# FFN up projection: two halves of the activations side by side in one 512-wide matmul per weight tile

## The reference

```python
def _swiglu(x, w1, w2):
    gt, up = jnp.split(x @ w1, 2, axis=-1)      # w1: 1024 x 5632
    return (jax.nn.silu(gt) * up) @ w2          # w2: 2816 x 1024

x = _layer_norm(DN_ALPHA * x + 0.5 * _swiglu(x, ffn1_w1[l], ffn1_w2[l]), ln1_g[l], ln1_b[l])
mix = _token_mix(x, ...)
x = _layer_norm(DN_ALPHA * x + mix, ...)
x = _layer_norm(DN_ALPHA * x + 0.5 * _swiglu(x, ffn2_w1[l], ffn2_w2[l]), ln3_g[l], ln3_b[l])
```

## Time and profile before

| | |
|---|---|
| time, median of 3 runs | 3143.65 us (3134.18 to 3158.1) |
| span of the profiled execution | 3151.0 us |
| PE busy | 2905.6 us, 92% |
| PE weight loads busy | 2683.1 us, 85% |
| POOL busy | 1948.4 us, 62% |
| ACT busy | 1181.7 us, 38% |
| DVE busy | 947.6 us, 30% |
| data moved | 491.20 MB, 156 GB/s on average |

### The profile page before, as it was taken

The page is one execution under the profiler, slowest core; times in us unless marked ns, Lnnn a source line. Parts: engine busy times, 40 slices in busy tenths (PEclk is TensorE's granted clock), DMA queues, the critical chain, the costliest instruction groups (busy, mean ns, idle before and its releaser), DMA issues.

```text
span 3151.0 us, 53968 instructions
## 1 busy us (share of the span) xinstructions
PE 2905.6 (92%) x19402; PEld 2683.1 (85%) x19402; DVE 947.6 (30%) x1581; ACT 1181.7 (38%) x1470; POOL 1948.4 (62%) x857
## 2 busy tenths in 40 slices
PE   5999979999899988999899899998989989999898
PEld 4997778899898878889889899887989989988797
DVE  2111273311211155511111222744121122374412
ACT  3443432344443443144344343314443434331444
POOL 5875451688785734178768774207877867421787
PEclk8999989999899999999899998999999999899999
DMA  6555432555554532355545444125555544413554
GB/s 209 183 173 177 138 101 81 195 187 188 173 187 154 191 118 98 103 197 185 174 159 187 153 162 150 66 95 186 185 176 170 185 150 158 152 61 107 181 187 155
DMA packets 131931, 491.20 MB, mean 156 GB/s; under 512 B 14657, under 2 KB 14657, under 8 KB 129633
## 3 DMA queue, kind: packets, MB, share of 16 engines
q1 hardware_dynamic: 128256, 467.10, 44.3%
q0 software_dynamic: 3424, 20.71, 1.8%
HBM read 485.63 MB, written 2.13 MB: 155 GB/s over the span
## 4 chain that ended last, share of the span: by engine, by line
PE 44%; issue 24%; POOL 23%; DVE 6%; ACT 2%; DMA 1%; POOLq 1%; DVEq 0%; ACTq 0%; SPq 0%
PE psA L356 28%; POOL rest L890 22%; PE psY L356 14%; PE psT L405 2%; DVE st L1080 1%; ACT Sc L1501 1%; DVE Sc L1085 1%; DVE xT_rest L1004 1%; POOLq L887 0%; ACT xT_upper L1501 0%; DVE Sc L1075 0%; DVE PT L1300 0%; DVE hT_upper L1062 0%; DMA cst<-in_consts 0%; DVE x L1047 0%
## 5 line engine op out<-in xcount | busy, mean ns | idle before, releaser
L890 POOL TENSOR_TENSOR rest<-ring,upper 128x1024 fp32r<-128x1024 f32 (+1 forms) x788 | 1906.6, 2425 | 1066.6 <-ACT upper L1501 1049.4
L1501 ACT ACTIVATE upper<-ring 128x1024 fp32r<-128x1024 f32 (+1 forms) x788 | 826.2, 1050 | 1117.8 <-PE psA L356 751.1
L356 PE MATMUL psA<-xT_upper,upper 128*128 128x256 f32 x3456 | 985.3, 285 | 16.8 <-DVE xT_rest L1004 12.8
L356 PE MATMUL psA<-xT_rest,upper 128*128 128x256 f32 x3456 | 983.9, 285 | 0.0
L356 PE MATMUL psA<-xT_upper,rest 128*128 128x256 f32 x3456 | 983.7, 285 | 0.0
L356 PEld LDWEIGHTS psA<-xT_upper,upper 128*128 128x128 f32 x3456 | 669.4, 194 | 27.8 <-issue 20.0
L356 PEld LDWEIGHTS psA<-xT_rest,upper 128*128 128x128 f32 x3456 | 669.3, 194 | 6.4
L356 PEld LDWEIGHTS psA<-xT_upper,rest 128*128 128x128 f32 x3456 | 668.9, 194 | 0.0
L1060 DVE TENSOR_TENSOR sil<-sil,psA 128x256 f32<-128x256 f32 x176 | 74.1, 421 | 1249.2 <-ACT sil L1501 1249.2
L356 PE MATMUL psY<-upper,hT_upper 128*128 128x512 f32 x704 | 277.2, 394 | 4.3 <-DVE hT_rest L1063 4.3
L356 PE MATMUL psY<-rest,hT_upper 128*128 128x512 f32 x704 | 277.1, 394 | 0.0
(11 more groups left out here) (223 smaller groups left out, 2959.8 us busy)
## 6 DMA issues: line engine op xcount, KB each, us to landing
ring<-in_weights SPq DMA_DIRECT2D x884, 512.0 KB, 3.3
G<-in_rows POOLq DMA_DIRECT2D x13, 1024.0 KB, 5.9
OT<-memory_transposed POOLq DMA_DIRECT2D x2, 1024.0 KB, 6.2
G<-rel_by_distance POOLq DMA_DIRECT2D x1, 2048.0 KB, 10.0
G<-in_mem SPq DMA_DIRECT2D x1, 1024.0 KB, 5.1
x<-in_x SPq DMA_DIRECT2D x1, 1024.0 KB, 11.0
memory_transposed<-arena POOLq DMA_DIRECT2D x1, 1024.0 KB, 6.8
par<-in_params POOLq DMA_DIRECT2D x4, 256.0 KB, 4.3
```

The lines of the kernel that those rows point to most:

```text
L356: i = pe.matmul(out, lhsT, rhs, start=start, stop=stop)
L890: pool.tensor_tensor(rest[:, r, 0:n], ring[:, r, 0:n], upper[:, r, 0:n], ALU.subtract)\
L1501: act.activation(out, in_, func, **kw).then_inc(*up)
```

## The change

`xT_upper` and `xT_rest` become the two halves of one tile, `xT_parts`, so that for a k-tile the 256 columns of each lie side by side. `up(j)` uses one bank for a and one for b: A0 and A1 for even j, T0 and T1 for odd j (T0 and T1 otherwise take transposes). For a k-tile, one matmul of 512 columns multiplies the weights' upper part with both halves: the left half of the bank gets upper x upper, the right half gets upper weights x rest of the activations. One matmul of 256 columns adds the weights' rest x the activations' upper part to the right half. Afterwards the halves are added: ACT copies the two right halves ("low sums") from PSUM to `halves_ab`, DVE adds the left halves to them, and silu and the product are taken from `halves_ab`.

The rest of the down pieces is no longer made by POOL (`down_piece` tells them) but by DVE, inside `hidden(f)`, between the additions and the product with silu. ACT splits the upper part of piece 3j + 4 between its low-sum copy and its silu. The size of a scratch area for POOL's own DMAs is set to 4096 bytes.

```diff
@@ PE, ffn()
                 def up(j):
-                    lab = ("ab", f, j)
-                    out = fill(pe, f"A{j % 2}", lab)
                     for v in range(2):
+                        lab = ("ab"[v], f, j)
+                        out = fill(pe, f"{'AT'[j % 2]}{v}", lab)
                         s = shaped(piece(), PIECE, "p (k c) -> p k c", k=KD)
                         for k in range(KD):
-                            product(out[:, v * S:(v + 1) * S], cut(s, ALL, k), cut(xT, ALL, k),
-                                    k == 0, k == KD - 1, filled(lab) if v == 1 and k == KD - 1 else None)
+                            mm(out, s[0][:, k], xT_parts[:, k, :, :], k == 0, False)
+                            mm(out[:, S:2 * S], s[1][:, k], xT[0][:, k], False, k == KD - 1,
+                               filled(lab) if k == KD - 1 else None)
                         free()
@@ which pieces DVE splits
+        def down_piece(h):
+            q = h % (PIECES - FFN_PIECES)
+            return (h < FFN_PIECES or AFTER_MIX <= h < PIECES) and (q == FFN_PIECES - 1 or q >= 4 and q % 3 == 1)
@@ POOL, split(h)
+                if down_piece(h):
+                    return
@@ DVE, hidden(f)
                 for j in range(FT):
-                    lab = ("ab", f, j)
+                    ab, v = halves_ab[:, j % 2], sil[:, j % 2, :]
+                    dve.wait_ge(*sig["low sums out"].after((f, j)))
+                    for n in range(2):
+                        lab = ("ab"[n], f, j)
+                        tt_(ab[:, n, :], at(lab)[:, 0:S], ab[:, n, :], ALU.add).then_inc(*read(lab))
+                    h = (0, AFTER_MIX)[f] + (3 * j + 4 if j < FT - 1 else FFN_PIECES - 1)
+                    dve.wait_ge(*sig["upper parts"].after(h))
+                    tt_(rest[:, h % R, :], ring[:, h % R, :], upper[:, h % R, :], ALU.subtract)\
+                        .then_inc(sig[f"place {h % R} emptied"].sem, 1)
+                    for n in range(2):
+                        dve.wait_ge(*taken(("ab"[n], f, j)))
                     dve.wait_ge(*sig["silu"].after((f, j)))
-                    v = sil[:, j % 2, :]
-                    tt_(v, v, at(lab)[:, S:2 * S], ALU.mult).then_inc(*read(lab))
-                    dve.wait_ge(*taken(lab))
+                    link(tt_(v, v, ab[:, 1, :], ALU.mult))
                     link(dve.tensor_copy(hT[0][:, j % 2, :], v))
                     tt_(hT[1][:, j % 2, :], v, hT[0][:, j % 2, :], ALU.subtract).then_inc(*sig["hidden"].up((f, j)))
@@ ACT, hidden(f)
                 for j in range(FT):
-                    lab = ("ab", f, j)
-                    until((0, AFTER_MIX)[f] + max(1, 3 * j))
-                    act.wait_ge(*full(lab))
+                    until((0, AFTER_MIX)[f] + 3 * j)
+                    for n in range(2):
+                        act.wait_ge(*full(("ab"[n], f, j)))
                     if j >= 2:
                         act.wait_ge(*sig["hidden"].after((f, j - 2)))
-                    go(sil[:, j % 2, :], at(lab)[:, 0:S], ACT.Silu, sig["silu"].up((f, j)))
+                    go(halves_ab[:, j % 2, :, :], pair(j)[:, :, S:2 * S], ACT.Copy, sig["low sums out"].up((f, j)))
+                    until((0, AFTER_MIX)[f] + min(3 * j + 1, FFN_PIECES - 1))
+                    act.wait_ge(*taken(("a", f, j)))
+                    go(sil[:, j % 2, :], halves_ab[:, j % 2, 0, :], ACT.Silu, sig["silu"].up((f, j)))
```

More of the change, by code:

```diff
@@ L172, in emit @@
         xn = sb("xn", [P, TT, D])
-        xT = (sb("xT_upper", [P, KD, S], F32R), sb("xT_rest", [P, KD, S], F32R))
+        xT_parts = sb("xT_parts", [P, KD, 2, S], F32R)
+        xT = (xT_parts[:, :, 0, :], xT_parts[:, :, 1, :])
         G = sb("G", [P, 24, S])
@@ L180, in emit @@
         sil = sb("sil", [P, 2, S])
+        halves_ab = sb("halves_ab", [P, 2, 2, S])
         hT = (sb("hT_upper", [P, 2, S], F32R), sb("hT_rest", [P, 2, S], F32R))
@@ L330, in width, with pair @@
             return PIECE if h >= PIECES else WIDTHS[places["made in"] == BLOCK2][h]
+        def down_piece(h):
+            q = h % (PIECES - FFN_PIECES)
+            return (h < FFN_PIECES or AFTER_MIX <= h < PIECES) and (q == FFN_PIECES - 1 or q >= 4 and q % 3 == 1)
+        def pair(j):
+            return (psA, psT)[j % 2]
         def parts_free(h):
@@ L1940 @@
     }
-    new = lambda: bacc.Bacc("TRN2", target_bir_lowering=False, num_devices=1)
+    new = lambda: bacc.Bacc("TRN2", target_bir_lowering=False, num_devices=1, dynamic_dma_scratch_size=4096)
     nc = new()
```

## The result

The changed kernel takes 3178.5 us (median of 8 runs, 3171.79 to 3189.01). The kernel before, run beside it, takes 3155.32 us (8 runs). The ratio is **1.0095, 95% interval 1.0076 to 1.0114**: slower by 1%, where no change was forecast. (The quotient of the two medians is 1.0073.) The profiled spans are 3176.9 and 3151.0 us. The forecast time of 3144 us stood on a median of 3 runs of the kernel before, 3143.65; the 8 runs beside the changed kernel have 3155.32. So of the 34.5 us between forecast and measured time, 11.7 are scatter of the kernel before; the change is 23.2, where 0.4 was forecast.

A forecast was written before the change was run, and what follows sets the result against it. The prediction took PE's matmul pace to bound the FFNs. Fewer matmuls (-36.6), tails (+3.2, +23.7, +7.2 of clock) and heads (+10.4, -7.5) summed to +0.4 us, giving 3144 us, range 3112 to 3176.

The forecast's parts named there:

- Term 1, fewer matmuls: Up projections: per k-tile one 512- and one 256-column matmul replace three of 256, saving 0.013 us each, 36.6 us less.
- Term 3, the heads: FFN starts, before down(0): two heads without table load lose 10.4 us, four lose nothing, two gain 7.5 us.
- Term 2, the tails: FFN ends, before down(21): PE waits 3.2 us over two tails, 23.7 over six where POOL gets in, plus 7.2 of clock.
- The steady part: Middle tiles of each FFN: the new chain ends before hidden(j) is due, so DVE, ACT and POOL do not become the bound.
- The slow parts: Low clock behind PE's waits: 7.2 us in six tails, bounds 0 and 14; 1.4 us per affected head, added or removed.
- the rival on the slower side: Six heads: DVE's last step starts after POOL's request, costing 5.2 us more each, 31.2 in all, 3175 us; chance 0.13.

The follow-up runs named there:

- e2_grouped: Changed kernel with each piece's matmuls reordered: first the eight of 512 columns, then the eight of 256; ratio 1.0047 to the kernel before.
- e7: Changed kernel with POOL's subtraction for one piece at the end of six FFNs cut to 8 of 1024 columns; profiled span 3162.0 us, one run.
- e8_table_early: Changed kernel with a one-column silu on spare data ahead of the wait for up(0), hiding the table load in six heads; profiled span 3187.2 us, one run.
- e3_chain_first: Changed kernel with silu ahead of ACT's down-piece split and DVE's hidden tile ahead of the down piece's rest; ratio 0.9944 to the kernel before.
- e1: Changed kernel with the rest of the down pieces made by POOL again instead of DVE; profiled span 3206.2 us, one run.

## Why the prediction was wrong

The forecast was +0.4 us on the span; it was +25.9, and +27.4 in the FFNs. Two steps failed.

- **Term 1, fewer matmuls: mis-sized.** Predicted 36.6 us less, measured 19.9 (176 x 0.113). The failed step is "The neighbours there run a 512 straight behind a 256 ... at the normal distances, so I take 36.6". In the records behind the earlier trace rows the first two matmuls of that down projection stand 0.233 and 0.236 us apart, not 0.227, and the rows themselves had 143.15 to 145.90 for the twelve, 2.75 us, 0.229 each. The prediction put 0.23 down to rounding. A switch of sizes costs some ns for a few matmuls, and the changed kernel switches at every matmul. e2_grouped shows it: in groups the same matmuls save 176 x 0.194 = 34.1 us, near the 36.6. The prediction had bounds of 0 and 36.6 for such a cost and took the upper one. By the Trainium skill (page "TensorE: Matmul & The Clock Gate", section "Back-to-back issue gap"), with 2.5 ns beside the columns, the term would be an estimated 7 us. The runs do not agree with it: in groups, where alternation costs next to nothing, the saving is 34.1. For the change as built the measured 19.9 lies between the two, 13 from the page's figure and 17 from the prediction's.
- **Term 3, the heads: a wait not looked for.** In the two heads without the table load the prediction was right: 3.13 us of wait (3.8 predicted), with 1.6 and 1.5 us of low clock behind it (1.4 predicted), and the cast is long; only DVE got its turn between POOL's two pieces, so it was long for one piece and the last step for the other. In the six others "DVE wins by 0.2 us and is in time: 0 us" was right for down(0), to the 0.2 us. But it stopped at tile 0: POOL, late by the same 1.28 us, meets tile 1, and down(1) waits 1.87 us in all six, 11.2 us and 1.6 of low clock in one. The 4.7 us of waits that two of these heads had before did go.
- **Term 2, the tails: right.** Predicted 3.2 + 23.7, measured 2 x 1.22 + 6 x 3.37 = 22.7, and 6.3 us of low clock (four of the six show 1.54 to 1.6) where 7.2 was taken. The mechanism, POOL getting in during DVE's subtraction, is in the rows above; e7 removes it alone. PE started 0.05 us behind hT_rest's end, not 0.35, which is a little more than half of the difference (8 x 0.3 of 4.2 us). The wrong detail: POOL got in ahead of the product, not the cast.
- **The steady part: right.** The chain ends in time and no tile waits.
- **The slow parts** rose by 11.8 us where 7.2 was taken (6 x 1.2 + 2 x 1.4 - 2 x 1.4); 2.4 of the difference is up(0)'s low clock, which scatters, and most of the rest a single longer distance (0.11 us) behind each wait.

Of the 27 us between forecast and account, 16.7 are term 1, 12.8 the waits ahead of down(1) with their clock, and 4.0 the slow parts just named; the tails give 5.1 back (4.2 of waits, 0.9 of clock) and the other heads 1.4. The direction of the rival on the slower side was right, its mechanism (DVE's last step losing the race by 0.2 us) was not what happened. It did happen in e8_table_early, where the request moved instead, at 3.0 to 3.1 us of wait a head.

## What to carry to other kernels

- A queue that keeps one engine fed has weak places at its ends, where what hides a wait is one short step instead of a tile. Work out a longer chain there, and follow it for two tiles, not one: what is late in the first is in the way of the second.
- When work is moved from a busy engine to an idle one, finish what the critical engine waits for first and put the moved work behind it. The same instructions in another order were worth 47 us here (e3_chain_first against the changed kernel), more than the matmuls that the change saved.
- Read distances in a timeline over a whole run of instructions. Two decimals hid 6 ns in 230, and 6 ns stood 2816 times in the sum. Keep matmuls of one size together.

## What the runs showed of the hardware

- Matmuls of 256 and 512 columns in turn run at 0.353 us a pair, in groups of eight at 0.347. Why a switch costs some ns is open.
- A DVE instruction with two SBUF inputs (0.42 us, 2.57 at 788.72), or an SBUF cast (0.29, 2.39 in e8), waits for a POOL subtraction that came first, and the reverse (POOL 2.40, 3.10 at 787.91). DVE's additions with one input in PSUM do not: all 352 in the changed kernel took 0.43 us or less, also beside a running POOL (58.55 and 58.89 in its first head). Where both wait, the other engine got its turn in most rows: POOL ahead of a DVE product that was already issued (788.72), and DVE between two POOL pieces (e1 at 144.68, e8 at 2196.75). In the earlier trace rows it did not: one cast waited 6.12 us through the ends of two POOL pieces. What decides this was not tried.
- Behind PE's waits the low clock (0.50) came in some cases and not in others of the same length: of the six tails with 3.37 us, four lose 1.5 to 1.6 us by it inside down(21) and two nothing, and of the six heads with 1.87 us one does. Windows of the changed kernel, behind the tail at 792.13 (us, then busy us and instructions of PE, PEld, DVE, ACT, POOL, then clock, DMA share, GB/s); 512-column matmuls start 0.427 us apart there, 0.227 elsewhere:

```profile
792.80:795.80 3.00, 3.00 (x9) 2.34 (x8) 1.38 (x2) 1.01 (x1) 1.92 (x1) 0.50 0.66 253
```
